# Hyena filters: the differences of the forward and backward halves move from VectorE to GpSimd

## The chip, the core and the metric

The kernel runs on one core of a Trainium2 chip. A core has TensorE (matmuls, called PE in the profile), VectorE (DVE), ScalarE (ACT), GpSimd (POOL) and SyncE (SP, which here only issues transfers), each with an instruction queue of its own. They meet through semaphores. The metric is the device time of one execution in microseconds (us); the median of three runs before the change is 2534.2.

## What is computed

One layer of a diffusion backbone on 1024 latent tokens with 1024 channels: a token mixer of four branches and a mixture of experts. The change touches the Hyena branch alone, and there the making of its long filters:

```python
hid = jnp.sin(lp["hy_freq"][1].astype(F32) * (hid @ lp["hy_w2"].astype(F32) + lp["hy_b2"].astype(F32)))
deltas = jnp.abs(jnp.linspace(HY_MIN_DECAY, HY_MAX_DECAY, HY_N_FILT, dtype=F32))
filt = (hid @ lp["hy_w3"].astype(F32)) * jnp.exp(-t01 * deltas)
filt = filt.reshape(n, HY_ORDER, 2, HY_D)
fwd, bwd = filt[:, :, 0], filt[:, :, 1]
k2 = jnp.concatenate([fwd, jnp.zeros((1, HY_ORDER, HY_D), F32), jnp.flip(bwd[1:], axis=0)], axis=0)
return k2 / jnp.sum(jnp.abs(k2), axis=0, keepdims=True)
```

The filters are multiplied in the frequency domain. The kernel needs, for every token tile and order, the sum fwd + bwd ("even") and the difference fwd - bwd ("odd"), which feed two kinds of matmuls against tables of cosines and sines, and the sum of magnitudes for the norm.

## The kernel before

The program is a row of stages. The first one, `stage_front`, makes the modulation vectors, the filters, their spectra, and then the Hyena branch's input projection. All later work stands behind it, on TensorE above all.

In the filter phase a *half* is one of 16 pairs of a token tile t (8 tiles of 128 tokens) and an order o (2). `halves` lists them in pairs (0,4), (0,4), (1,5), (1,5) and so on, so that the first 8 halves hold the tiles 0, 4, 1 and 5. What each engine does, in its own order:

- TensorE: `filters(2j)` makes halves 2j and 2j+1 (8 passes of 512 columns, L539) into PSUM, of which three halves fit (`filt_read`). After each pair come two `modulation` items (L524, 512 KB of weights each from a ring of four slots), which wait for the ScalarE copy of the items before (`mod_read`). After every second pair come the magnitude sums of four halves (`magnitudes`, L560), which wait for ScalarE's magnitudes (`mags_ready`). After the last pair, 16 small matmuls turn the modulation rows (L625), and the block sums of the spectra follow (L547): first four matmuls on odd of tiles 4, 5, 0 and 1, then the fourth magnitude sum, then the rest.
- ScalarE: for each half the magnitudes (L697), which wait for VectorE's product (`filt_ready`) and for the magnitude sums of the four halves before (`summed`); after every even half one decay window (L681), after every odd half a copy of modulation rows (L674).
- VectorE: for each half the product of PSUM and the decay window, 128x1024 (L795), into one of four slots of `filt`; then even and odd, 128x512 each, both from that slot (L806). A slot is free for half n when magnitudes n-4 and both results of half n-4 are there. For tile 0 a 128x512 multiply (L800) comes between, which sets row 0 of bwd to zero.
- GpSimd: a memset at the start, and later the stores of seven of the eight spectrum units (L477). In the filter phase it does nothing.
- SyncE: loads, among them x into the memory of the windows, which waits for all 16 products.

The order is written out by hand, nothing schedules it. `ps`, `sb_uT` and `sb_spare` in the profile are PSUM, the decay windows and the tiles `filt` and `mags`; `front_even` and `front_odd` are the results.

Of the kernel before, what the change touches and what calls it, by code (L numbers as in the profile page):

```python
# [24 lines left out]
ALU = mybir.AluOpType  # L25
# [382 lines left out]
def stage_front(k, q_tok, scratch, base_at):  # L408
# [3 lines left out]
    nc, a, ring, ps = k.nc, k.a, k.ring, k.ps  # L412
# [4 lines left out]
    halves = [(tiles[2 * j + s], o) for j in range(TT // 2) for o in range(2) for s in range(2)]  # L417
# [4 lines left out]
    with k.stage("front") as (sb, sem):  # L422
        sb("arena", [P, 25 * kilo // 4])

        def at(name, kb, shape, dt=F32):
            return placed(nc, f"front_{name}", shape, dt, base_at + int(kb * kilo))

        even, odd = at("even", 0, [P, TT, 2, HY_D]), at("odd", 32, [P, TT, 2, HY_D])
# [12 lines left out]
        filt = k.spare[:, 0:4, :].rearrange("p b (d c) -> p b d c", d=2)  # L441
# [9 lines left out]
        pre_ready, arg_ready, hid_ready = sem("pre_ready"), sem("arg_ready"), sem("hid_ready")  # L451
        filt_mm, filt_read, window_ready = sem("filt_mm"), sem("filt_read"), sem("window_ready")
        filt_ready, folded, mags_ready, summed = sem("filt_ready"), sem("folded"), sem("mags_ready"), sem("summed")
        sum_read = sem("sum_read")
        ones_set, filter_dve, mod_read, mod_turned, mod_done = (sem(x) for x in (
            "ones_set", "filter_dve", "mod_read", "mod_turned", "mod_done"))
# [16 lines left out]
        def store(eng, n, done):  # L473
            kt, comp, o = units[n]
            eng.wait_ge(spec_ready, 2 * n + 2)
            for h in range(CH_HALVES):
                eng.dma_start(a["spectra"][(o * CH_HALVES + h) * KTILES + kt, :, comp, :, :],  # L477
                              spec[:, n % 2, :, h * HALF_C:(h + 1) * HALF_C]).then_inc(done, 16)
# [15 lines left out]
        with nc.Block() as block:  # L494
            @block.sync
            def _(sp):
                sp.dma_start(cc[:, :, :], a["ccT"]).then_inc(cc_in, 16)
                for dst, src in ((featT[:, :], a["featT"]), (w1[:, :], a["hy_w1"]), (k.cols[:, :], a["cols"]),
                                 (w2[:, :], a["hy_w2"])):
                    sp.dma_start(dst, src).then_inc(feat_in, 16)  # L500
                sp.dma_start(w3[:, :], a["hy_w3"]).then_inc(w3_in, 16)
                sp.dma_start(k.consts[:, :], a["consts"]).then_inc(consts_in, 16)
                sp.dma_start(deltas[:, :], a["neg_deltas"][0].partition_broadcast(P)).then_inc(deltas_in, 16)
                sp.dma_start(bias[:, :, :].rearrange("p o c -> p (o c)"),
                             a["rows"][:, ROW_AT["hy_bias"][0]:ROW_AT["hy_bias"][1]]).then_inc(bias_in, 16)
                ring.stream(sp)
                sp.wait_ge(filt_read, len(halves))
                sp.dma_start(k.uT[:, :, :], a["xT"].rearrange("(k p) t -> p k t", p=P)).then_inc(x_in, 16)
                ring.stream(sp)
                store(sp, len(units) - 1, last_stored)  # L510
                ring.stream(sp)
                stored_all(sp)

            @block.tensor
            def _(pe):
# [28 lines left out]
                def block_sum(n, bank, slot, first, of):  # L544
                    kt, comp, o = units[n]
                    for i, t in enumerate(of):
                        mm = nc.tensor.matmul(ps[:, 4 * (n % 2) + bank, :],  # L547
                                              ring.buf[:, slot, (first + i) * P:(first + i + 1) * P],
                                              (even, odd)[comp][:, t, o, :], start=(i == 0), stop=(i == len(of) - 1))
                    return mm  # L550

                def magnitudes(g):

                    pe.wait_ge(ones_set, 1)
                    pe.wait_ge(mags_ready, 4 * g + 4)
                    for s in range(2):
                        for o in range(HY_ORDER):
                            for d in range(2):
                                q = 2 * o + d
                                mm = nc.tensor.matmul(ps[q * COLS:(q + 1) * COLS, 7, :], k.ones[:, 0:COLS],  # L560
                                                      mags[:, 2 * o + s, d, :], start=(g == 0 and s == 0),
                                                      stop=(g == 3 and s == 1))
                    mm.then_inc(summed, 1)

                def norms():
                    pe.wait_ge(sum_read, 1)
                    pe.wait_ge(picked, 3)
                    for o in range(HY_ORDER):
                        nc.tensor.matmul(ps[0:1, 4 + o, :], pick_o[:, o:o + 1], mag_sum[:, :], start=True, stop=True)
                        for m in range(HM):  # L570
                            mm = nc.tensor.matmul(ps[:, 7, o * HM + m:o * HM + m + 1], mag_sum[:, m * P:(m + 1) * P],
                                                  pick_o[:, o:o + 1], start=True, stop=True)
                    mm.then_inc(norm_mm, 1)
# [55 lines left out]
                for n in range(len(units)):  # L629
                    slot, last = 2 * (n // HY_ORDER % 2), n % HY_ORDER == HY_ORDER - 1  # L630
                    if n == 0:
                        pe.wait_ge(folded, len(halves))
                        pe.wait_ge(filt_read, len(halves) - 2)
                    elif n == 1:
                        pe.wait_ge(norm_read, 3)
                        pe.wait_ge(mod_done, 1)
                    else:
                        pe.wait_ge(sums_read, n - 1)
                    if n == 2:
                        pe.wait_ge(bias_added, 1)  # L640
                    ring.arrived(pe, dft_base, n // RING, slot)
                    block_sum(n, 3, slot, 2, (4, 5))
                    block_sum(n, 2, slot, 0, (0, 1))
                    if n == 0:
                        pe.wait_ge(folded, 2 * len(halves))
                        magnitudes(3)
                    mm = block_sum(n, 0, slot, 4, (2, 3, 6, 7))
                    if last:
                        mm.then_inc(ring.freed, 1)
                    if n == 0:  # L650
                        norms()
                    ring.arrived(pe, dft_base, n // RING, slot + 1)
                    block_sum(n, 1, slot + 1, 0, (2, 3, 6, 7)).then_inc(ring.freed if last else sums_mm, 1)
# [100 lines left out]
            @block.gpsimd  # L754
            def _(pool):
                nc.gpsimd.memset(cc_wide[:, :, :], 0.0).then_inc(wide_blank, 1)
                for n in range(len(units) - 1):
                    store(pool, n, stored[n % 2])

            @block.vector  # L760
            def _(v):
                tt = nc.vector.tensor_tensor
# [25 lines left out]
                for n, (t, o) in enumerate(halves):  # L788
                    mine, spot = filt[:, n % 4, :, :], tiles.index(t)
                    v.wait_ge(filt_mm, n + 1)  # L790
                    v.wait_ge(window_ready, spot + 1)
                    if n >= 4:
                        v.wait_ge(mags_ready, n - 3)
                        v.wait_ge(folded, 2 * (n - 3))
                    tt(mine, ps[:, 2 * (n % 3):2 * (n % 3) + 2, :],  # L795
                       window[:, spot % 4, 2 * o * HY_D:2 * (o + 1) * HY_D].rearrange("p (d c) -> p d c", d=2),
                       ALU.mult).then_inc(filt_read, 1)
                    v.wait_ge(filt_read, n + 1)
                    if t == 0:
                        nc.vector.tensor_scalar(mine[:, 1, :], mine[:, 1, :], k.const("not_first", 0, 1), None,  # L800
                                                ALU.mult).then_inc(filt_ready, 1)
                        v.wait_ge(filt_ready, n + 1)
                    else:
                        v.sem_inc(filt_ready, 1)
                    for dst, op in ((even, ALU.add), (odd, ALU.subtract)):
                        tt(dst[:, t, o, :], mine[:, 0, :], mine[:, 1, :], op).then_inc(folded, 1)  # L806
                v.wait_ge(folded, 2 * len(halves))
                v.wait_ge(mod_turned, 1)
                ch.step(tt(k.mod[:, :, :], ps[:, 6, 0:2 * EARLY].rearrange("p (m r) -> p m r", r=2),
                           k.col("b_mod", 0, EARLY).unsqueeze(2).broadcast_to([P, EARLY, 2]), ALU.add))  # L810
# [33 lines left out]
                for m in range(n_hy):  # L844
                    src, dst = line[:, m % 2, :], conv[:, m % 2, :]
# [2602 lines left out]
```

## Time and profile before

| what | value |
|---|---|
| median of three runs | 2534.2 us (2533.22 to 2534.28) |
| the profiled execution | 2533.14 us, of which the span 2531.3 |
| TensorE busy | 2388.0 us, 94% of the span |
| VectorE busy | 1631.4 us, 64% |
| ScalarE busy | 940.4 us, 37% |
| GpSimd busy | 276.5 us, 11% |

The span runs from the first to the last instruction, and all times of the trace count from its start. A share of busy time is a mean over stages of different kinds; what the filter phase is bound by has to be read in its own stretch, 22 to 67 us. A timeline row gives start, duration, engine, line, operation, output and inputs, shapes, a count where equal rows were merged, and in brackets the idle time before it with what ended it. A fp32 matmul shows as two passes.

### The profile page before, as it was taken

The numbers are of one execution on the slowest core, as the hardware profiler recorded it, in microseconds if no ns is written. First come the engines' busy times: TensorE is split into PE (matmuls) and PEld (weight loads), VectorE is DVE, ScalarE is ACT, GpSimd is POOL, SyncE is SP. The second block draws the span as 40 slices with busy tenths as digits, with TensorE's granted clock in tenths as the row PEclk, the third lists the DMA queues.
The fourth block names the chain that finished last, engine by engine and source line by source line (L and its number), as shares of the span: only waits on it lengthen the run. The fifth ranks groups of instructions, "written<-read, shape, count | busy, mean of one in ns | idle before, by whom it ended". The sixth has DMA issues, their size and how long they took to land. (4 is left out here: it accounts for less than half of the span.)

```text
span 2531.3 us, 30519 instructions
## 1 busy us (share of the span) xinstructions
PE 2388.0 (94%) x11945; PEld 1927.1 (76%) x11945; DVE 1631.4 (64%) x1685; ACT 940.4 (37%) x1097; POOL 276.5 (11%) x268
## 2 busy tenths in 40 slices
PE   6999899899999999999999999999599999999994
PEld 2468778678877878788787788868588888888882
DVE  7453388633343755324975437578888888888876
ACT  5133311233323533001112000031277777777764
POOL 0000000000143400000000001100012122121210
PEclk9999999999999999999999999999699999999997
DMA  5431154312345313111111115533699999999965
GB/s 203 173 117 42 66 188 171 103 46 84 119 147 156 98 50 108 49 44 50 42 50 38 42 50 179 175 136 117 269 363 362 370 360 363 361 372 387 386 266 204
DMA packets 93966, 437.11 MB, mean 173 GB/s; under 512 B 17432, under 2 KB 28968, under 8 KB 79146
## 3 DMA queue, kind: packets, MB, share of 16 engines
q1 hardware_dynamic: 64714, 349.02, 37.5%
q0 software_dynamic: 29152, 86.69, 9.8%
q8 instruction: 70, 1.15, 0.2%
q14 instruction: 30, 0.25, 0.0%
HBM read 401.12 MB, written 55.51 MB: 180 GB/s over the span
## 5 line engine op out<-in xcount | busy, mean ns | idle before, releaser
L390 PE MATMUL ps<-uT_upper_rest,ring_rest 128*128 128x512 f32 x1280 | 504.7, 394 | 0.0
L390 PE MATMUL ps<-uT_upper_rest,mix_upper 128*128 128x512 f32 x768 | 307.4, 400 | 9.9 <-DVE mix_val L2424 5.3
L390 PE MATMUL ps<-uT_rest,mix_upper 128*128 128x512 f32 x768 | 306.3, 399 | 0.0
L390 PEld LDWEIGHTS ps<-uT_upper_rest,ring_rest 128*128 128x128 f32 x1280 | 240.6, 188 | 61.0
L390 PEld LDWEIGHTS ps<-uT_upper_rest,mix_upper 128*128 128x128 f32 x768 | 145.4, 189 | 47.6 <-DVE mix_val L2424 5.7
L390 PEld LDWEIGHTS ps<-uT_rest,mix_upper 128*128 128x128 f32 x768 | 145.3, 189 | 33.0 <-issue 0.5
L1856 ACT ACTIVATE mix_gates<-ps 128x1024 f32<-128x1024 f32 x24 | 24.7, 1028 | 385.8 <-PE ps L390 368.8
L1907 DVE TENSOR_TENSOR mix_prod<-mix_gates,ps 128x1024 f32<-128x1024 f32 x24 | 29.3, 1221 | 212.4 <-PE ps L390 212.4
L2955 PE MATMUL ps<-ex_u_raw_rest,uT_rest 128*128 128x256 f32 x560 | 157.0, 280 | 0.0
L2953 PE MATMUL ps<-ring_rest,uT_rest 128*128 128x256 f32 (+1 forms) x416 | 135.1, 325 | 3.1 <-DVE uT_rest L3318 2.4
L2953 PE MATMUL ps<-ex_upper,uT_rest 128*128 128x256 f32 (+1 forms) x424 | 134.9, 318 | 0.0
L2954 PE MATMUL ps<-ex_upper,uT_rest 128*128 128x256 f32 (+1 forms) x424 | 134.1, 316 | 0.0
L2954 PE MATMUL ps<-ring_rest,uT_rest 128*128 128x256 f32 (+1 forms) x416 | 133.3, 320 | 0.0
L390 PE MATMUL ps<-uT_upper_rest,ssd_upper 128*128 128x512 f32 x320 | 129.0, 403 | 0.0
L390 PE MATMUL ps<-uT_rest,ssd_upper 128*128 128x512 f32 x320 | 127.1, 397 | 0.0
L2843 POOL DMA_INDIRECT y_rows<-sb_uT,ex_scatter_at x35 | 91.9, 2625 | 293.4 <-ACT sb_uT L3072 293.0
L390 PE MATMUL ps<-mix_y_upper,mix_upper 128*128 128x512 f32 x288 | 115.1, 400 | 1.8 <-DVE mix_y_bT_rest L398 1.8
L390 PE MATMUL ps<-mix_y_upper,ring_rest 128*128 128x512 f32 x288 | 112.6, 391 | 0.0
L2955 PE MATMUL ps<-merged_rest,ex_hid_up 128*128 128x512 f32 x280 | 110.7, 396 | 0.0
L2955 PE MATMUL ps<-uT_upper_rest,uT_rest 128*128 128x512 f32 x280 | 110.7, 395 | 0.0
L2955 PEld LDWEIGHTS ps<-ex_u_raw_rest,uT_rest 128*128 128x128 f32 x560 | 105.3, 188 | 0.0
L2439 DVE SCALAR_TENSOR_TENSOR mix_y_aT<-mix_val,sb_cols,mix_y_aT 128x64 f32<-128x64 f32 (+14 forms) x120 | 90.2, 752 | 4.1
(477 smaller groups left out, 5502.0 us busy)
## 6 DMA issues: line engine op xcount, KB each, us to landing
sb_spare<-in_ex_g SPq DMA_DIRECT2D x35, 2048.0 KB
ex_u_raw<-in_ex_u SPq DMA_DIRECT2D x35, 2048.0 KB, 10.2
sb_merged<-in_ex_d SPq DMA_DIRECT2D x35, 2048.0 KB
ring<-in_conv SPq DMA_DIRECT2D x32, 512.0 KB, 3.3
ring<-in_w_gate SPq DMA_DIRECT2D x32, 512.0 KB, 3.4
mix_piece<-in_w_late POOLq DMA_DIRECT2D x32, 512.0 KB, 5.4
ring<-in_w_ssd SPq DMA_DIRECT2D x20, 512.0 KB, 3.3
ring<-in_w_mod SPq DMA_DIRECT2D x16, 512.0 KB, 4.5
```

The source lines that it names most:

```text
L390: last = self.nc.tensor.matmul(out, weight, x[:, k, lo:hi], start=(k == 0 and n == 0), stop=(k == kt - 1 and n == 2))
L1856: nc.scalar.activation(gate_of(i), both(gate_bank(i)), ACT.Sigmoid).then_inc(gate_ready, 1)
L1907: nc.vector.tensor_tensor(mine if first else prod[:, :], gate_of(i), both(gate_bank(i) + 2), ALU.mult).then_inc(prod_ready, 1)
L2439: ins = nc.vector.scalar_tensor_tensor(out=acc[:, lo:hi], in0=val[:, t, lo + s * GRID_W:hi + s * GRID_W], scalar=weight, in1=acc[:, lo:hi] ...
L2843: pool.indirect_dma_start(out=a["y_rows"], out_offset=bass.IndirectOffsetOnAxis(scatter_at[:, i:i + 1], 0), in_=y, in_offset=None, bounds_ ...
L2953: nc.tensor.matmul(out, left_up, w_up, start=first, stop=False)
L2954: nc.tensor.matmul(out, left_lo, w_up, start=False, stop=False)
L2955: return nc.tensor.matmul(out, left_up, w_lo, start=False, stop=last)
```

## The change

GpSimd gets a loop over the 16 halves. Each turn waits for the product of its half and writes odd. VectorE keeps the products and the sums. A new semaphore `odd_folded` counts the differences, `folded` now counts the sums alone. VectorE's product n waits for difference n-4 (the sums stand before it on its own engine); TensorE's first block sum waits for eight differences, its fourth magnitude sum for all sixteen of each.

```diff
+        odd_folded = sem("odd_folded")
...
                     if n == 0:
-                        pe.wait_ge(folded, len(halves))
+                        pe.wait_ge(odd_folded, len(halves) // 2)
                         pe.wait_ge(filt_read, len(halves) - 2)
...
                     if n == 0:
-                        pe.wait_ge(folded, 2 * len(halves))
+                        pe.wait_ge(odd_folded, len(halves))
+                        pe.wait_ge(folded, len(halves))
                         magnitudes(3)
...
                 nc.gpsimd.memset(cc_wide[:, :, :], 0.0).then_inc(wide_blank, 1)
+                for n, (t, o) in enumerate(halves):
+                    pool.wait_ge(filt_ready, n + 1)
+                    nc.gpsimd.tensor_tensor(odd[:, t, o, :], filt[:, n % 4, 0, :], filt[:, n % 4, 1, :],
+                                            ALU.subtract).then_inc(odd_folded, 1)
...
                         v.wait_ge(mags_ready, n - 3)
-                        v.wait_ge(folded, 2 * (n - 3))
+                        v.wait_ge(odd_folded, n - 3)
...
-                    for dst, op in ((even, ALU.add), (odd, ALU.subtract)):
-                        tt(dst[:, t, o, :], mine[:, 0, :], mine[:, 1, :], op).then_inc(folded, 1)
-                v.wait_ge(folded, 2 * len(halves))
+                    tt(even[:, t, o, :], mine[:, 0, :], mine[:, 1, :], ALU.add).then_inc(folded, 1)
+                v.wait_ge(folded, len(halves))
```

VectorE, halves 4 to 6 of the filter phase, in the kernel before, in the order of its queue:

```order
L795 TENSOR_TENSOR sb_spare<-ps,sb_uT 128x1024 [waits front_mags_ready,front_folded,front_window_ready,front_filt_mm]
L806 TENSOR_TENSOR front_even<-sb_spare 128x512 [waits front_filt_read]
L806 TENSOR_TENSOR front_odd<-sb_spare 128x512
L795 TENSOR_TENSOR sb_spare<-ps,sb_uT 128x1024 [waits front_mags_ready,front_folded,front_window_ready,front_filt_mm]
L806 TENSOR_TENSOR front_even<-sb_spare 128x512 [waits front_filt_read]
L806 TENSOR_TENSOR front_odd<-sb_spare 128x512
```

The same place of VectorE in the changed kernel:

```order
L801 TENSOR_TENSOR sb_spare<-ps,sb_uT 128x1024 [waits front_mags_ready,front_odd_folded,front_window_ready,front_filt_mm]
L811 TENSOR_TENSOR front_even<-sb_spare 128x512 [waits front_filt_read]
L801 TENSOR_TENSOR sb_spare<-ps,sb_uT 128x1024 [waits front_mags_ready,front_odd_folded,front_window_ready,front_filt_mm]
L811 TENSOR_TENSOR front_even<-sb_spare 128x512 [waits front_filt_read]
L801 TENSOR_TENSOR sb_spare<-ps,sb_uT 128x1024 [waits front_mags_ready,front_odd_folded,front_window_ready,front_filt_mm]
L811 TENSOR_TENSOR front_even<-sb_spare 128x512 [waits front_filt_read]
```

One instruction in three has left the queue, and the product waits for GpSimd's semaphore instead of VectorE's own.

GpSimd at the start of the program, in the changed kernel (before, the memset of front_cc_wide is followed directly by the stores of the spectra, which now stand behind these rows):

```order
L758 MEMSET front_cc_wide 128x256
L761 ISA
L761 TENSOR_TENSOR front_odd<-sb_spare 128x512 [waits front_filt_ready] x16
L478 DMA spectra<-front_spec 128x4x256 [waits front_spec_ready]
L478 DMA spectra<-front_spec 128x4x256
```

The row ISA is the load of GpSimd's library for such operations; before, it stood ahead of the first GpSimd product of a later stage (L1632).

## Rows read from the trace of the kernel before

**Rows 1.** The page, busy times of the engines, with their share of the span.

```profile
PE 2388.0 (94%) x11945; PEld 1927.1 (76%) x11945; DVE 1631.4 (64%) x1685; ACT 940.4 (37%) x1097; POOL 276.5 (11%) x268
```

**Rows 2.** Groups of instructions, 20 to 110 us: busy, mean ns, idle before.

```profile
L806 DVE TENSOR_TENSOR front_odd<-sb_spare 128x512 f32<-128x512 f32 x16 | 10.9, 684 | 0.0
```

**Rows 3.** Timeline of VectorE, 19 to 69 us.

```profile
41.56 1.23 DVE L795 TENSOR_TENSOR sb_spare<-ps,sb_uT 128x1024 f32<-128x1024 f32 x1 [1.39 <-PE ps L539]
...
52.35 1.22 DVE L795 TENSOR_TENSOR sb_spare<-ps,sb_uT 128x1024 f32<-128x1024 f32 x1
...
57.53 1.22 DVE L795 TENSOR_TENSOR sb_spare<-ps,sb_uT 128x1024 f32<-128x1024 f32 x1
58.90 0.69 DVE L806 TENSOR_TENSOR front_even<-sb_spare 128x512 f32<-128x512 f32 x1 [0.16 <-DVE sb_spare L795]
59.51 0.69 DVE L806 TENSOR_TENSOR front_odd<-sb_spare 128x512 f32<-128x512 f32 x1
60.11 1.22 DVE L795 TENSOR_TENSOR sb_spare<-ps,sb_uT 128x1024 f32<-128x1024 f32 x1
61.49 0.69 DVE L806 TENSOR_TENSOR front_even<-sb_spare 128x512 f32<-128x512 f32 x1 [0.16 <-DVE sb_spare L795]
```

**Rows 4.** Timeline of ScalarE, 19 to 69 us.

```profile
33.97 1.04 ACT L697 ACTIVATE sb_spare<-sb_spare 128x1024 f32<-128x1024 f32 x1
...
53.66 1.06 ACT L697 ACTIVATE sb_spare<-sb_spare 128x1024 f32<-128x1024 f32 x1 [0.55 <-DVEq L804]
...
59.74 1.06 ACT L697 ACTIVATE sb_spare<-sb_spare 128x1024 f32<-128x1024 f32 x1 [1.93 <-PE ps L560]
61.42 1.06 ACT L697 ACTIVATE sb_spare<-sb_spare 128x1024 f32<-128x1024 f32 x1 [0.62 <-DVEq L804]
62.38 0.35 ACT L674 COPY front_mod_rows<-ps 128x256 f32<-128x256 f32 x1
```

**Rows 5.** Timeline of TensorE's matmuls, 19 to 82 us.

```profile
35.16 2.75 PE L560 MATMUL ps<-sb_spare,sb_ones 128*32 128x512 f32 x16 [2.55 <-ACT sb_spare L697]
...
39.55 1.99 PE L539 MATMUL ps<-front_w,front_hid 64*128 64x512 f32 x8
...
49.65 1.99 PE L539 MATMUL ps<-front_w,front_hid 64*128 64x512 f32 x8
...
54.27 1.99 PE L539 MATMUL ps<-front_w,front_hid 64*128 64x512 f32 x8
57.70 1.92 PE L560 MATMUL ps<-sb_spare,sb_ones 128*32 128x512 f32 x16 [1.45 <-ACT sb_spare L697]
...
60.43 1.99 PE L539 MATMUL ps<-front_w,front_hid 64*128 64x512 f32 x8
62.79 3.73 PE L625 MATMUL ps<-front_pick,front_mod_rows 128*128 128x2 f32 x32 [0.37 <-ACT front_mod_rows L674]
...
71.69 1.92 PE L560 MATMUL ps<-sb_spare,sb_ones 128*32 128x512 f32 x16
```

**Rows 6.** Line L1632 on GpSimd over the whole span: durations in ns, library load.

```profile
L1632 POOL TENSOR_TENSOR ssd_xend<-ssd_xs,sb_dt_dt_to_end x18: 1462/1468/2447, 713.3 to 879.7; 128x768 f32<-128x768 f32 x18
L1632 POOLq MODIFY_POOL_CONFIG  x2: 74/74/74, 710.0 to 710.0; - x2
```

**Rows 7.** Timeline of VectorE, 865.9 to 868.4 us.

```profile
866.02 0.96 DVE L1585 TENSOR_TENSOR ssd_grow_f<-ssd_grow_f,ssd_grow_b 128x768 f32<-128x768 f32 x1 [0.18 <-ACT ssd_grow_b L1447]
867.15 0.95 DVE L1590 TENSOR_TENSOR ssd_grow_f<-ssd_grow_f,ps 128x768 f32<-128x768 f32 x1 [0.17 <-PE ps L1332]
```

**Rows 8.** Timeline of GpSimd in the same stretch.

```profile
866.25 2.06 POOL L1693 TENSOR_TENSOR ssd_skip<-ssd_xs,ssd_d_row 128x768 f32<-128x768 f32 x1 [0.59 <-PE ps L1311]
```

**Rows 9.** Timeline of VectorE, 713 to 720 us, beside the first L1632 of GpSimd.

```profile
713.11 1.29 DVE L1500 SCALAR_TENSOR_TENSOR sb_merged<-sb_merged,sb_cols 128x1024 f32<-128x1024 f32 x1
714.44 2.38 DVE L1503 SCALAR_TENSOR_TENSOR sb_merged<-sb_merged,sb_cols 128x1024 f32<-128x1024 f32 x1
```

**Rows 10.** Timeline, 60 to 110 us: VectorE's last write of a unit, GpSimd's store.

```profile
87.77 1.22 DVE L831 TENSOR_TENSOR front_spec<-front_pair,ps 128x1024 f32<-128x1024 f32 x1
...
89.30 1.75 POOL L477 DMA_DIRECT2D spectra<-front_spec  x2 [88.25 <-DVE front_spec L831]
```

**Rows 11.** Stretch 35 to 41.5 us: busy times, granted clock, DMA share, GB/s.

```profile
35.00:41.50 6.50, 6.34 (x56) 3.01 (x56) 4.86 (x6) 3.76 (x5) 0.00 (x0) 0.74 0.24 79
```

## The prediction, made before the changed kernel ran

> **What bounds the kernel now.** I read the page's busy times first: TensorE is busy for 94% of the span [rows 1], so the end moves by what TensorE's first steps move by, unless a later wait swallows it. The change lies in the filter phase, which in the trace runs from 22.8 to 66.4 us. There I read the timelines of VectorE, ScalarE and TensorE side by side, and looked in each row for the idle time before it and its releaser. A half is one of the 16 (token tile, order) pairs; I number them 0 to 15, with product n, even n, odd n for VectorE's three steps and Abs n for ScalarE's magnitude step.
>
> From half 8 on VectorE is the engine that never rests. The product starts at 57.53, even 58.90, odd 59.51, next product 60.11 [rows 3]: a pitch of 2.58 us, of which odd takes 0.60 (0.68 by its own duration, overlapped by its successor) [rows 2]. The step that sets the end is the row L625 at 62.79 on TensorE, the turning of the modulation rows [rows 5]. It waits for the ScalarE copy at 62.38, that one stands behind Abs 13 at 61.42, and Abs 13 waits 0.62 us for product 13 of VectorE, which starts at 60.11 [rows 3, 4]. From L625 on TensorE runs without a gap into the block sums at 66.4 and beyond.
>
> But VectorE sets this time only in part. Product 6 at 41.56 waited 1.39 us for TensorE [rows 3], whose filter matmuls at 39.55 stand behind the magnitude sums at 35.16, and these waited for Abs 3 at 33.97, which has no idle time before it: ScalarE was full [rows 4, 5]. So everything that VectorE gains before 41.56 is lost there again.
>
> **What the change removes from VectorE, and what remains of it.** 16 x 0.60 = 9.6 us leave VectorE. Its pitch when nothing else holds it becomes 2.58 - 0.60 = 1.98 us. Following the chain:
> - Products 0 to 5 come up to 1.8 us earlier, product 6 stays at 41.56, since the TensorE and ScalarE rows before it don't move. Gain so far: none.
> - Product 7 gains 0.60, but Abs 7 and the magnitude sums behind it are held by ScalarE. Filter matmuls 8 and 9 stand behind the TensorE rows that haven't moved.
> - Filter matmuls to product takes 41.56 - 39.55 = 2.01 us [rows 3, 5]. So product 10 can start at 49.65 + 2.01 = 51.66, before it was 52.35, and ends at 52.88. Abs 10 waited 0.55 us for it at 53.66 [rows 4]; this wait is what goes, and no more, for ScalarE is free only at 53.11.
> - Abs 11 and the magnitude sums at 57.70 follow by 0.55, to 57.15; Abs 12 from 59.74 to 59.19; filter matmuls 14 and 15 from 60.43 to 59.88 [rows 4, 5].
> - Product 12: filter matmuls at 54.27 stand still, so 54.27 + 2.01 = 56.28 (it was 57.53). Product 13: 56.28 + 1.98 = 58.26, end 59.48. Abs 13 follows Abs 12 directly, 59.19 + 0.97 = 60.16 (it was 61.42), the copy at 61.12, its end and the release 0.41 later, 61.53.
> - L625 now waits for TensorE itself: the filter matmuls at 59.88 end between 61.60 (8 passes of 0.215) and 61.87 (their 1.99). I take 61.75 against 62.79: **gain 1.04 us**. What is late next is TensorE and ScalarE with 2.0 to 2.1 us of work a half each.
>
> **What it adds.** Sixteen GpSimd subtractions of 128x512. The trace has none of this shape; the nearest is the 128x768 product at L1632, 1.47 us [rows 6]. By columns that is 0.98, and the whole 1.47 is the upper end; I take 1.0, since the short fixed part can't be large. GpSimd does nothing in this stretch but wait: its next row is the spectrum store at 89.30, which waits for VectorE [rows 10]. At 1.0 or 1.47 it keeps up with a pitch of 1.98. [...]
>
> The GpSimd library load (the MODIFY_POOL_CONFIG rows, at 710.0 in this trace with the first product 3.3 us later [rows 6]) moves to the program's start, where GpSimd has nothing to do until product 0 at 22.8: nothing. Even a late odd 0 would be harmless for a while, as product 4, four halves on, is the first to wait for it.
>
> New waits: product n waits for odd n-4 (over 6 us of slack). The first block sum waits for odd 7 (done by about 47, needed at 65). The fourth magnitude sum, at 71.69 before, waits for odd 15 [rows 5]: product 15 at 59.88 + 2.01 + 1.98 = 63.87, odd 15 done near 66.9, needed at 70.65. Its cover is 3.7 us. The load of x on the SP queue waits for product 15 and comes some 1.4 us earlier; ScalarE first uses it in the third unit of the block sums, so it stays hidden.
>
> [...] Even n and odd n are now released by the same product, and both read the same tile. The trace shows that VectorE and GpSimd obstruct each other where both have their inputs in SBUF: the GpSimd row at 866.25 took 2.06, against 1.47 for the one at L1632, and the VectorE row at 866.02 with two SBUF inputs, which began 0.23 earlier, kept its 0.96 [rows 6, 7, 8]. The other way round, the VectorE row at 714.44 began while GpSimd worked and took 2.38 instead of 1.29 us [rows 9]. A VectorE row with an input in PSUM, as the product has, kept its 0.95 beside GpSimd (867.15) [rows 7]. So the later of the two pays, and what counts is who starts first. Even starts 0.16 after the product's end. ScalarE, released by the same semaphore as GpSimd will be, starts after 0.09 (61.33 to 61.42) [rows 3, 4]. GpSimd's store starts 0.31 after VectorE's last write (89.30 against 88.99) [rows 10]. I take GpSimd's start between these and nearer to the store's, about 0.2: VectorE first, by a hair. Then odd waits some 0.6 and runs beside the next product, at no price.
>
> [...]
>
> **The sum.** Profiled execution: span 2531.3, with 1.84 around it 2533.14. Less 1.04: 2532.1. The median of the three runs is 2534.2, 1.06 above the profiled one; taken from there, **2533.2 us**. A measurement tells some 0.2% (5.1 us) from no change, so this is no change that can be told.
>
> **Rivals.**
> A. GpSimd first (it ends on the slow side). Odd starts 0.09 after the product, even waits for its end. At 1.0 us even begins at 1.09 instead of 0.16: lost 0.93, saved 0.60, the pitch is 2.91, 0.33 more than before. From product 6 to 13 that is 7 x 0.33 = 2.3 us, and all of it arrives, since VectorE is then the last; the 4 x 0.33 = 1.3 of halves 2 to 5 lie within the 1.39 us that product 6 waited [rows 3]: 2536.5. With 1.47 us the pitch is 0.80 more: 7 x 0.80 = 5.6, and halves 2 to 5 bring 4 x 0.80 = 3.2, of which the 1.39 us that product 6 waited [rows 3] cover a part; 1.8 is left: 2541.6. It passes 5.1 us from a GpSimd time of about 1.26 us. For it: ScalarE's 0.09 is less than 0.16. Against it: the store's 0.31.
> B. Nothing arrives at the end: a later wait of TensorE on a transfer swallows the microsecond. For it: TensorE's 6% of idle time. Against it: later transfers are released by TensorE or VectorE, and move along. 2534.2.
> [...]
> D. The gain is larger, with ScalarE's rows not as full as I take them: at most 7 x 0.60 = 4.2 from product 6 to 13, 2530.0.
>
> **How the numbers follow.** Forecast 50%, A 28% (of it the part beyond 5.1 us 7%), B 10%, C 8%, D 4%. The range takes in the forecast, B, C, and A up to about 1.2 us of GpSimd time: 2530.8 to 2538.5. Faster by over 0.2% would need more than D: 3%. Slower by over 0.2%: the end of A, 8%. Within: 89%.
>
> **What would show it.** Right: product 6 near 41.6, product 13 near 58.3, L625 near 61.75, even with 0.69 and odd recorded at 1.5 to 1.7 (wait included) in the steady stretch. Rival A: even at 1.4 to 1.7 us, odd at 1.0, VectorE's pitch near 2.9, L625 near 65. B: L625 early and the span not. [...] The prediction is wrong at its root if products 10 to 13 don't come earlier though even kept its duration, for then ScalarE or TensorE hold all of it.

## The result and the profile after

The changed kernel is slightly slower: its median is 2539.11 us (20 runs), that of the kernel before beside it 2534.26; the ratio is 1.0016 with a 95% interval of 1.0010 to 1.0023. That is 2.5 to 5.8 us more. By the bound of 0.2% it is no change that one measurement can tell, as forecast, but it lies on the other side from the forecast (-1.0 us) and above the range. Two of the twenty executions of the kernel before took 3689 and 5022 us, a slow state that the ratio leaves out. The profiled execution took 2540.11 us, 7.0 more than the profiled one of before.

The page of the changed kernel, busy times; they answer to [rows 1]:

```profile
PE 2391.5 (94%) x11945; PEld 1928.3 (76%) x11945; DVE 1636.5 (64%) x1669; ACT 941.2 (37%) x1097; POOL 300.8 (12%) x284
```

VectorE lost 16 instructions and is busy for 5 us *longer*. Where that is shows in its timeline in the changed kernel, from half 6 on, against [rows 3]:

```profile
41.43 1.23 DVE L801 TENSOR_TENSOR sb_spare<-ps,sb_uT 128x1024 f32<-128x1024 f32 x1 [0.46 <-PE ps L540]
42.81 1.80 DVE L811 TENSOR_TENSOR front_even<-sb_spare 128x512 f32<-128x512 f32 x1 [0.16 <-DVE sb_spare L801]
...
53.81 1.21 DVE L801 TENSOR_TENSOR sb_spare<-ps,sb_uT 128x1024 f32<-128x1024 f32 x1
55.18 1.80 DVE L811 TENSOR_TENSOR front_even<-sb_spare 128x512 f32<-128x512 f32 x1 [0.16 <-DVE sb_spare L801]
56.90 1.21 DVE L801 TENSOR_TENSOR sb_spare<-ps,sb_uT 128x1024 f32<-128x1024 f32 x1
...
63.07 1.21 DVE L801 TENSOR_TENSOR sb_spare<-ps,sb_uT 128x1024 f32<-128x1024 f32 x1
```

The sum (even) takes 1.80 us where it took 0.69, and the pitch of a half is 56.90 - 53.81 = 3.09 where it was 2.58. GpSimd's timeline in the same stretch:

```profile
55.16 1.27 POOL L761 TENSOR_TENSOR front_odd<-sb_spare 128x512 f32<-128x512 f32 x1 [1.82 <-DVEq L810]
```

The subtraction starts at 55.16, the sum at 55.18. The product had ended at 53.81 + 1.21 = 55.02, so GpSimd needs 0.14 us from VectorE's signal, and VectorE 0.16 from its own product's end. GpSimd is ahead by 0.02, goes through undisturbed, and the sum stands still until the subtraction is nearly done. So it goes in all thirteen halves from half 3 on, with GpSimd 0.02 or 0.03 ahead. In halves 0 and 2, where VectorE's zeroing step (L806) releases both, the sum is ahead (24.66 against 24.71 us in half 0) and keeps its 0.69; the subtraction waits instead. In half 1 GpSimd comes late, from its subtraction before. The two starts are recorded 0.01 apart, and the sum keeps its 0.69 here too, though GpSimd's start is the earlier one by that 0.01:

```profile
26.62 1.83 POOL L761 TENSOR_TENSOR front_odd<-sb_spare 128x512 f32<-128x512 f32 x1
```

```profile
26.63 0.69 DVE L811 TENSOR_TENSOR front_even<-sb_spare 128x512 f32<-128x512 f32 x1
```

A recorded start is thus not quite the moment that decides: GpSimd won where it was 0.02 ahead, not where it was 0.01 ahead.

The modulation rows are turned (L626) at 65.75 instead of 62.79 [rows 5], on TensorE's timeline of the changed kernel, and TensorE now comes to it without an idle time that the profile shows:

```profile
59.41 2.88 PE L561 MATMUL ps<-sb_spare,sb_ones 128*32 128x512 f32 x16 [2.35 <-ACT sb_spare L699]
61.98 1.90 PE L525 MATMUL ps<-ring,front_cc_wide 128*32 128x128 f32 x32
63.82 1.99 PE L540 MATMUL ps<-front_w,front_hid 64*128 64x512 f32 x8
65.75 3.73 PE L626 MATMUL ps<-front_pick,front_mod_rows 128*128 128x2 f32 x32
```

VectorE's product 13 sets this time still: from its start to the turning it is 2.68 us, as before (63.07 to 65.75, 60.11 to 62.79). TensorE's own rows end at nearly the same moment, since its clock was partly at the lower level there (0.50 from 61 to 63 us, 0.62 over the 4.5 us of the two rows, 1.00 for the same rows before): after an idle time of 2.35 us the magnitude sums took 2.88 instead of 1.92 and the modulation items 1.90 instead of 1.08. All three traces of the changed kernel have this (magnitude sums of 2.88, 3.49 and 2.99), those of the kernel before don't (1.92). It costs nothing at the turning, because TensorE would have waited there for product 13 anyway.

Of the 7.0 us between the two profiled spans, 2.96 stand at the turning. Another 1.7 come between L626 and the first projection matmul, which starts at 160.8 instead of 156.2: TensorE was granted 0.83 of its full clock from 80 to 90 us, a mix of 1.00 (to 84 us and from 88) and 0.50 (85 to 87), where the kernel before had 1.00. The view by stretch, of the changed kernel first and then of the one before:

```profile
80.00:90.00 10.00, 10.00 (x32) 4.62 (x31) 2.62 (x5) 0.59 (x1) 0.00 (x0) 0.83 0.24 95
```

```profile
80.00:90.00 10.00, 10.00 (x30) 4.99 (x30) 6.21 (x8) 0.58 (x1) 0.70 (x1) 1.00 0.01 2
```

The last 2.4 us come in the rest of the program, which took 2377.5 us from that matmul on, against 2375.1 before. Neither of the two is in every execution of the changed kernel: two more traces of it (experiments 4 and 9) have the clock at 1.00 from 75 to 95 us, and 2375.0 and 2373.7 us for the rest. But those two executions took 2536.14 and 2534.56 us, where their medians are 2540.0 and 2538.3, so they don't show what a usual one loses.

### The profile page after: what moved, and what is told of

Read it like the earlier page. It is cut to its first block and busy times, and to the rows that moved or that the text cites. A ratio compares the mean times of both kernels' runs of the same rounds, so it can differ in the third digit from the quotient of the medians.

```text
span 2538.3 us, 30520 instructions
## 1 busy us (share of the span) xinstructions
PE 2391.5 (94%) x11945; PEld 1928.3 (76%) x11945; DVE 1636.5 (64%) x1669; ACT 941.2 (37%) x1097; POOL 300.8 (12%) x284
```

## The experiments

The measure that hardly scatters is the time from the start of product 6 to the turning of the modulation rows. It is 21.23 us before (41.56 to 62.79) and 24.32 after (41.43 to 65.75).

**1. The subtraction waits for the sum.**

```diff
-                    pool.wait_ge(filt_ready, n + 1)
+                    pool.wait_ge(folded, n + 1)
```

> The changed kernel with one wait moved: GpSimd's subtraction waits for VectorE's sum of the same half (folded) instead of for its product, so that it can no longer start ahead of the sum. [...] Rival (GpSimd's work beside VectorE costs time in whatever order, by contention with the products too): products longer than 1.22, L626 at 64 or later, time near 2538.

Measured: 2533.52 us against 2533.94 before, ratio 0.9999 (0.9991 to 1.0008). VectorE and TensorE in this kernel:

```profile
57.11 1.23 DVE L801 TENSOR_TENSOR sb_spare<-ps,sb_uT 128x1024 f32<-128x1024 f32 x1 [0.57 <-PE ps L540]
58.49 0.69 DVE L811 TENSOR_TENSOR front_even<-sb_spare 128x512 f32<-128x512 f32 x1 [0.16 <-DVE sb_spare L801]
59.10 1.22 DVE L801 TENSOR_TENSOR sb_spare<-ps,sb_uT 128x1024 f32<-128x1024 f32 x1
```

```profile
60.61 1.99 PE L540 MATMUL ps<-front_w,front_hid 64*128 64x512 f32 x8
62.52 3.73 PE L626 MATMUL ps<-front_pick,front_mod_rows 128*128 128x2 f32 x32
```

The sum is back at 0.69 and the pitch at 1.99; the product, with one operand in PSUM, keeps its 1.22 beside a subtraction of 1.28. Product 6 to L626 takes 20.14 us (42.38 to 62.52), 1.09 less than before; the prediction had worked out 1.04 for "VectorE first". L626 is at 62.52 and not at the prediction's 61.75 because this execution came to product 6 0.8 us later; it had lost them by product 2 (30.12 against 29.34). The rival's figures (products longer than 1.22, L626 at 64 or later, 2538) didn't come. The 5 us by which the changed kernel was slower are gone. GpSimd's subtraction has an undisturbed row here, with VectorE idle from 50.63 to 52.49:

```profile
50.71 1.28 POOL L761 TENSOR_TENSOR front_odd<-sb_spare 128x512 f32<-128x512 f32 x1 [0.74 <-DVE front_even L811]
```

**2. The same pitch without GpSimd.** Left out of the diff: the buffer and the semaphore, and a later wait of ScalarE before it uses that memory.

```diff
+                    if n >= 3:
+                        tt(idle[:, 0:400], mine[:, 0, 0:400], mine[:, 1, 0:400], ALU.add).then_inc(idle_set, 1)
```

> The kernel before, GpSimd untouched; VectorE gets one more addition of 128x400 in each half from half 3 on (into memory that nobody reads), some 0.50 us by 0.61 for 512 columns. VectorE's pitch is then 3.08, that of the changed kernel (3.09). Theory (all that the change costs, the 4 us behind L626 included, comes from VectorE's longer pitch in the filter phase): L625 near 65.7, and a time like the changed kernel's, 2537 to 2540. Rival (the part behind L626, which is 4 of the 7 us of the profiled spans, comes from GpSimd: its library loaded at another place, its queue, other instruction code): L625 near 65.7 too, but a time of 2536 to 2537, 3 above before and no more.

```profile
50.53 1.22 DVE L798 TENSOR_TENSOR sb_spare<-ps,sb_uT 128x1024 f32<-128x1024 f32 x1
51.91 0.69 DVE L809 TENSOR_TENSOR front_even<-sb_spare 128x512 f32<-128x512 f32 x1 [0.16 <-DVE sb_spare L798]
52.52 0.68 DVE L809 TENSOR_TENSOR front_odd<-sb_spare 128x512 f32<-128x512 f32 x1
53.12 0.57 DVE L811 TENSOR_TENSOR front_idle<-sb_spare 128x400 f32<-128x400 f32 x1
53.60 1.22 DVE L798 TENSOR_TENSOR sb_spare<-ps,sb_uT 128x1024 f32<-128x1024 f32 x1
```

VectorE's pitch is 3.07, product 6 to the turning 24.18 us, 2.95 more than before. The time is 2537.5 us, ratio 1.0014 (1.0005 to 1.0023), 3.5 us above before. So a longer pitch of VectorE is enough for most of what the change costs, with no work on GpSimd at all. One thing is different from the changed kernel: TensorE stands idle before the turning, and the turning itself runs partly at the lower clock (0.50 from 69 to 75 us, 1.00 before 68):

```profile
65.50 4.12 PE L627 MATMUL ps<-front_pick,front_mod_rows 128*128 128x2 f32 x32 [1.59 <-ACT front_mod_rows L676]
```

It takes 4.12 us instead of 3.73, the first block sums behind it 6.67 instead of 5.38. That is 1.7 us of the clock's, on top of the 2.95.

**3. The library load alone.** One GpSimd memset and one subtraction on spare memory, at the program's start. Left out of the diff: the buffer, the semaphore and a wait of ScalarE, as in experiment 2.

```diff
+                nc.gpsimd.memset(idle[:, :], 0.0).then_inc(idle_set, 1)
+                pool.wait_ge(idle_set, 1)
+                nc.gpsimd.tensor_tensor(idle[:, :], idle[:, :], idle[:, :], ALU.subtract).then_inc(idle_set, 1)
```

> The kernel before, with one GpSimd memset and one subtraction of 128x512 at the program's start, on memory that nobody reads, which moves the load of GpSimd's library from 710 us to the start, as the change does. If the moved load costs or gives anything, the time moves here by itself; the theory says nothing moves: L625 at 62.8, time as before within 0.05%. The rival of the last run would see up to 4 us more. The subtraction runs alone, so its own time shows: 1.1 to 1.3 us.

```profile
L762 POOLq MODIFY_POOL_CONFIG  x2: 11/11/11, 1.5 to 1.5; - x2
L762 POOL TENSOR_TENSOR front_idle<-front_idle x1: 1037/1037/1037, 1.6 to 1.6; 128x512 f32<-128x512 f32 x1
```

Ratio 0.9998 (0.9990 to 1.0007), product 6 to the turning 21.22 us. The turning stood at 63.76 and not at the expected 62.8, since product 6 came 0.98 later. The moved load costs nothing that these runs can tell, and nothing is gained by it where it was: the first GpSimd product of the later stage came no earlier (713.6 us, [rows 6] 713.3). The subtraction follows the load by 0.1 us. Alone, with one tile as both inputs and as its output, it took 1.04 us, less than the 1.1 to 1.3 expected and than the 1.27 in the changed kernel.

**4. The changed kernel beside these three.**

> The changed kernel again, on the chip of the three others, to compare with them: ratio to before 1.0010 to 1.0025, L626 at 65.75, even 1.80 us, GpSimd's subtraction 1.27.

2540.0 us (7 runs), ratio 1.0025 (1.0014 to 1.0036), product 6 to L626 24.33 us. L626 was at 65.97. Its profiled span is 2534.4, though, 3.9 below the first profile of the same kernel: from 75 to 95 us the clock stayed at 1.00, and the first projection matmul started at 159.4 instead of 160.8. The profiled execution (2536.14 us) was the fastest of the seven.

**5. GpSimd writes, but doesn't read.**

```diff
-                    nc.gpsimd.tensor_tensor(odd[:, t, o, :], filt[:, n % 4, 0, :], filt[:, n % 4, 1, :],
-                                            ALU.subtract).then_inc(odd_folded, 1)
+                    nc.gpsimd.memset(odd[:, t, o, :], 0.5).then_inc(odd_folded, 1)
```

> The changed kernel, but GpSimd fills odd with a constant (memset, 128x512) instead of subtracting; it leaves the differences out. Released by the same product, it starts as early as the subtraction, and writes the same memory, but reads nothing. Theory (what holds the sum up is the read of two tiles in SBUF): even 0.69 us, VectorE's pitch 2.0 where nothing else holds it, from product 6 to L626 20.1 to 20.3 us (before 21.2, after 24.3). Rival (any GpSimd instruction on SBUF, or its writes, hold VectorE's sum up): even 1.1 us or more.

The timelines of GpSimd and VectorE in one half:

```profile
53.48 0.52 POOL L761 MEMSET front_odd<- 128x512 f32 x1 [2.97 <-DVEq L809]
```

```profile
53.52 0.69 DVE L810 TENSOR_TENSOR front_even<-sb_spare 128x512 f32<-128x512 f32 x1 [0.16 <-DVE sb_spare L800]
```

GpSimd is ahead by 0.04 us, as the subtraction was by 0.02 to 0.03, and runs for three quarters of the sum's time; the sum keeps 0.69. Product 6 to L626: 20.17 us. The one execution took 2532.52 us. So a GpSimd instruction beside the sum doesn't obstruct it as such, nor does writing the same memory: the memset, which reads nothing, left the sum at 0.69, the subtraction, which reads two tiles, held it to 1.80.

**6. Half the width.** GpSimd subtracts 256 of the 512 columns.

```diff
+                nc.gpsimd.memset(odd[:, :, :, 256:512], 0.5)
...
-                    nc.gpsimd.tensor_tensor(odd[:, t, o, :], filt[:, n % 4, 0, :], filt[:, n % 4, 1, :],
+                    nc.gpsimd.tensor_tensor(odd[:, t, o, 0:256], filt[:, n % 4, 0, 0:256], filt[:, n % 4, 1, 0:256],
```

> The changed kernel with GpSimd's subtraction cut to 256 of 512 columns (the other half of odd is a constant, set once at the start, and so left out). Theory (the sum waits for the end of the whole subtraction): GpSimd 0.7 us by 1.27 x 256/512 and a fixed part, even 0.69 + 0.5 = 1.2 us, pitch 2.5, product 6 to L626 20.2 to 20.8. Rival (a fixed price for each meeting of the two, whatever its size): even 1.8 us as before, pitch 3.1.

```profile
51.31 0.73 POOL L762 TENSOR_TENSOR front_odd<-sb_spare 128x256 f32<-128x256 f32 x1 [1.82 <-DVEq L811]
```

```profile
51.33 1.26 DVE L812 TENSOR_TENSOR front_even<-sb_spare 128x512 f32<-128x512 f32 x1 [0.16 <-DVE sb_spare L802]
```

The subtraction is 0.54 shorter (0.73 for 1.27), and the sum's extra time falls by the same 0.54, from 1.11 to 0.57. Reckoned back from its end, the sum's own 0.69 us begin 0.14 us before the subtraction's end at both widths. So the sum waits for nearly the whole of the subtraction, at either length. Product 6 to L626: 20.55 us; the one execution took 2530.07 us.

**7. Two lines of VectorE exchanged.** The signal for the other engines goes behind the sum in VectorE's program.

```diff
-                    else:
-                        v.sem_inc(filt_ready, 1)
                     tt(even[:, t, o, :], mine[:, 0, :], mine[:, 1, :], ALU.add).then_inc(folded, 1)
+                    if t:
+                        v.sem_inc(filt_ready, 1)
```

> The changed kernel with two lines of VectorE's program exchanged: the signal that releases GpSimd and ScalarE (filt_ready) is given after the sum is issued, not before. Nothing else is moved, and the two still run at the same time. Theory (the 0.03 us by which GpSimd starts ahead decide everything): the sum is first, even 0.69, GpSimd's subtraction recorded at 1.7 to 1.9 with its wait, pitch 2.0 to 2.1, product 6 to L626 20.2 to 20.6, time 2533 to 2535. If the signal is given only when the sum has ended, the subtraction starts 0.6 us later and is recorded at 1.27, with the same pitch. Rival (with both running at the same time the sum always yields): even 1.8, pitch 3.1, time 2539.

VectorE and GpSimd in one half:

```profile
52.23 1.23 DVE L801 TENSOR_TENSOR sb_spare<-ps,sb_uT 128x1024 f32<-128x1024 f32 x1 [1.57 <-PE ps L540]
53.48 0.69 DVE L809 TENSOR_TENSOR front_even<-sb_spare 128x512 f32<-128x512 f32 x1
54.09 1.22 DVE L801 TENSOR_TENSOR sb_spare<-ps,sb_uT 128x1024 f32<-128x1024 f32 x1
```

```profile
53.60 1.73 POOL L761 TENSOR_TENSOR front_odd<-sb_spare 128x512 f32<-128x512 f32 x1 [1.80 <-DVEq L811]
```

The same two instructions meet again, with the order reversed: the sum starts 0.12 ahead and keeps 0.69, the subtraction waits and is recorded at 1.73. So it is in all 16 halves (durations in ns, minimum, median and maximum):

```profile
L809 DVE TENSOR_TENSOR front_even<-sb_spare x16: 691/692/693, 25.5 to 65.5; 128x512 f32<-128x512 f32 x16
```

```profile
L761 POOL TENSOR_TENSOR front_odd<-sb_spare x16: 1708/1716/1787, 25.5 to 65.6; 128x512 f32<-128x512 f32 x16
```

The signal is given when the sum starts, not when it ends. It stands for the product, which VectorE has waited for before, and doesn't say that the sum is done; that has its own semaphore (`folded`). The sum also starts 0.02 instead of 0.16 after the product, since the signal no longer stands between them; the pitch is 1.86. Product 6 to L626 takes 20.20 us. The time is 2532.85 (10 runs), ratio 0.9994 (0.9984 to 1.0004).

**8. The kernel before again.**

> The kernel before once more, for a second trace of it: how much of the differences between single traces is scatter. By the traces so far I expect L625 between 62.8 and 63.8, product 6 to L625 21.2 within 0.2, and the first projection matmul (156.2 in the first trace) up to 2 us later or not, by whether TensorE's clock falls between 75 and 95 us.

Product 6 to L625 is 21.23 us to the hundredth, but product 6 stood at 39.65 instead of 41.56: the magnitude sums (1.92 us for 2.75) and the modulation items (1.08 for 2.01) before it ran at the higher clock (1.00 over the two rows, 34.72 to 37.70; in the first trace 0.67 from 35.16 to 37.91, and 0.50 from 37 to 39). TensorE in this second trace, and its clock, against [rows 5] and [rows 11]:

```profile
34.72 1.92 PE L560 MATMUL ps<-sb_spare,sb_ones 128*32 128x512 f32 x16 [2.24 <-ACT sb_spare L697]
```

```profile
35.00:41.50 6.50, 4.87 (x73) 2.44 (x69) 6.03 (x8) 4.70 (x5) 0.00 (x0) 1.00 0.47 175
```

One and the same kernel differs by 1.9 us here between two executions, before the stretch of the change is reached. The one execution took 2530.89 us. The expectation of 62.8 to 63.8 for L625 was missed for that reason (60.88).

**9 to 12. More runs of the two slow kernels, twice the delay, and the better kernel once more**, all on one chip.

> The changed kernel again, beside the longer-VectorE kernel on one chip, to settle whether the time behind L626 belongs to the longer pitch or to GpSimd. By the runs so far 2539 to 2540; 3.1 us of it stand at L626 in each trace. Theory (the rest comes with the delay, in whatever way it is made): the two kernels' times agree within 1 us in this job. Rival (GpSimd has a price of its own later on): this one 1.5 us or more above the next.

Measured: 2538.3 us, ratio 1.0016 (1.0006 to 1.0027); L626 at 65.70, 24.32 us behind product 6; span of the profiled execution 2532.8.

> The kernel before with the 128x400 addition in each half again, pitch 3.07 without GpSimd. Theory: as the changed kernel within 1 us. Rival: 2536 to 2537.5, which is the kernel before plus its 2.95 us from product 6 to L625, and nothing more.

Measured: 2536.92 us, ratio 1.0011 (1.0003 to 1.0020), 1.4 below the changed kernel. That is on the rival's side of the 1 us and short of its 1.5: no decision. The turning again ran partly at the lower clock (0.50 from 68 to 71 us):

```profile
65.44 5.43 PE L627 MATMUL ps<-front_pick,front_mod_rows 128*128 128x2 f32 x32 [1.60 <-ACT front_mod_rows L676]
```

> The same with two such additions in each half, VectorE's pitch 3.55. If a delay at L625 arrives at the end as it is: product 6 is itself late by some 1.6 us, then 7 x 0.96 = 6.7 more, so L625 at about 71 and a time 8.3 us above before, near 2542.5. If a delay is multiplied on its way (4.85 at the end for 3.0 at L626, as in the changed kernel): 13 us above, near 2547.

VectorE's pitch was 3.56 (54.14 to 57.70), L625 at 71.05, 8.3 us behind the first trace of before. The time is 2545.82 (5 runs), ratio 1.0046 (1.0033 to 1.0059), 8.4 to 15 us above before, and lies between the two expectations. The turning took 4.74 us here, after an idle time of 1.13 and with the clock at 0.50 from 74 us on, and it is 95.05 us to the first projection matmul instead of 93.40.

> The changed kernel with VectorE's signal behind its sum, more rounds: whether it beats the kernel before. From product 6 to L626 it took 20.2 against 21.2 us, so I expect a ratio of 0.9996 with an interval on both sides of 1, or just under it; its ten times so far gave 0.9994 (0.9984 to 1.0004).

2533.05 us (12 runs), ratio 0.9989 (0.9980 to 0.9999). Together with its first ten runs (0.9994) the kernel with the exchanged lines lies 1.5 to 3 us below the one before by the two ratios, of which 1.0 is shown in the traces. The first interval takes in 1, the second ends just below it. It is the best version here, by less than one measurement can tell.

## Why the prediction was wrong, point by point

- **The bound and the path** were right. The filter phase gives its time to the end through product 13, Abs 13, the copy and the turning of the modulation rows. With VectorE's pitch at 3.09, L626 moved by 2.96 us and the median by more than that; with the pitch at 1.99 L626 came 1.09 earlier, counted from product 6.
- **What remains of 9.6 us**, worked out as 1.04, was right where its condition held: 1.09 in experiment 1, 1.06 in experiment 5, 1.03 in experiment 7. Its 0.215 us for a filter pass is in the trace: in the kernel before the matmuls of this row start at 60.43, 60.97, 61.39 and 61.83, two passes each, so 0.43 apart but for the first step of 0.54. TensorE and ScalarE absorb the rest, as the chain over products 10, 12 and 13 had it: product 12 waits for TensorE in all three kernels (0.57 us in experiment 1).
- **Who starts first: the step that failed.** The prediction put GpSimd's start at about 0.2 us after the product's end, from the 0.31 us of a store, and so VectorE first, by 0.04. It is 0.14, and VectorE's own wait lasts 0.16. ScalarE's 0.09 in [rows 4] was the nearer row, because it is released by the same signal; the store's 0.31 is that of a DMA issue, another kind of instruction. The forecast hung on a margin of some 0.04 us between estimates 0.2 apart, and 50% to 28% was more than they carried.
- **Rival A** is what happened: even at 1.80, VectorE's pitch near 3, L626 near 65. It was priced too low, at 2.3 us with a subtraction of 1.0. The subtraction took 1.27. With that, the pitch grows by 1.11 - 0.60 = 0.51, and 7 x 0.51 = 3.6. Of that the trace before had spent 0.4 already, in one long half (3.01 us from product 7 to 8): 3.1, as measured. What rival A added for halves 2 to 5 didn't come: product 6 stood at 41.43 (41.56 before) and still waited 0.46 us for TensorE, for the sum was held up in halves 3 to 5 only. The row of 768 columns scaled to 0.98 by columns; the kernel's own subtraction needed 30% more. The fixed part is short, as the prediction took it: 0.73 us at 256 columns and 1.27 at 512 leave 0.19, by an estimate. That the subtraction takes 1.27 isn't VectorE's doing: the one at 50.71 in experiment 1 took 1.28 with VectorE idle. With a single tile as both inputs and output it took 1.04 (experiment 3); whether the second tile makes the difference, or the place in memory, no run separates.
- **How the two obstruct each other** was read rightly from [rows 6, 7, 8, 9], and the runs bear it out for the sum and the subtraction: the sum, started second, waits for nearly the whole subtraction (1.80 for 0.69; experiment 6: its delay shrinks with the subtraction, 0.54 for 0.54), a GpSimd memset that only writes doesn't hold it up (0.69, experiment 5), the product with an input in PSUM keeps its 1.22 (experiment 1), and the order decides who waits (experiment 7: sum 0.69, subtraction 1.73), to within the 0.01 us of half 1. Both read the same tile in all these kernels, but that isn't what obstructs: in [rows 7, 8, 9] the tiles are different. What the prediction got wrong was the order.
- **The library load** was right at nothing (experiment 3). The new waits were covered, as said: VectorE's product never waited for GpSimd.
- **TensorE's clock** (C among the chances, 8%; no run shows how often it decides the time) goes different ways in one kernel, and only in part by the change. Between two executions of the kernel before product 6 and the turning lie 1.9 us apart, 1.8 of them in the rows that ran at different clocks (experiment 8). From the turning to the first projection matmul eight of the fourteen traces take 93.39 or 93.40 us. Three take 95.09 or 95.10, each with 0.83 of the clock granted from 80 to 90 us: the changed kernel's first trace but not its two others, experiment 1 and the second trace of the exchanged lines. These 1.7 us come and go in one and the same kernel. The three traces with a longer VectorE pitch take 95.02, 96.77 and 95.05, with the slower turning shown above in each. Tied to the change are the slower magnitude sums before the turning, which were hidden.
- **The size left open.** By the ratios, the changed kernel was 4.1, 6.3 and 4.1 us above before in its three sets of runs, 3.1 of it at L626. The kernel with the longer VectorE was 3.5 and 2.8 above, 2.95 of it there, and its traces lose 1.6 or more after that to the clock. Whether GpSimd has a further price of 1 us or so, or a late turning costs more by the clock on its way (twice the delay gave 8.4 to 15 for 8.3), isn't settled. The executions without a trace speak for the clock. A mean granted clock of 0.972 or less stands in 26 of 39 executions of the changed kernel, in 18 of 23 with the longer pitch and in 5 of 5 with twice the addition, the last two without GpSimd; in the kernel before it is 19 of 73, with the exchanged lines 5 of 22, in experiment 1 4 of 11. No run held the clock fixed, so this is a hint and not shown.
- **The range** ended at 2538.5 and missed the time by 0.6. The 3.1 us at L626 alone would have given 2537.3, inside it; what put the time outside is the part left open. It took in rival A only up to a subtraction of 1.2 us.

## What to carry to other kernels

A step given to GpSimd that reads SBUF while VectorE reads two tiles from there wasn't free work beside it here. Whichever started second waited for nearly the whole of the other (the sum took 1.80 us for 0.69, with the lines exchanged the subtraction 1.73 for 1.27), and where both are released by the same event, some hundredths of a microsecond decided which it was (0.02). Issue the critical engine's instruction first and signal the other behind it: two exchanged lines took away the 4 us here (ratios 0.9994 and 0.9989 to the kernel before). A signal so placed is right only for what was finished before that instruction, as the product was here. And before anything is moved off the busiest engine, follow the chain to see how much arrives: of 9.6 us one arrived.

## What the runs showed of the hardware

- GpSimd started 0.12 to 0.14 us after a signal of VectorE, ScalarE 0.09, and VectorE 0.16 after its own product, if a signal stands between; 0.02 where none does (experiment 7).
- A signal placed behind an instruction in VectorE's program was given when that instruction started: GpSimd started 0.12 after the sum's start, 0.57 before its end.
- The first GpSimd subtraction followed the load of its library, recorded as MODIFY_POOL_CONFIG, by 0.1 us (experiment 3: 1.5 and 1.6).
- A subtraction of 128x512 on GpSimd took 1.27 us in these kernels where it didn't wait, with VectorE at work or idle, 0.73 at 256 columns (experiment 6), and 1.04 where both inputs and the output were the same tile (experiment 3).
